# Streaming encoder step, one core: half of w_out reloaded once per tile, two more ring slots for U and two for V

## What is computed

```python
# per layer
x = x + concat([mlstm(q, k, v, gates), sliding_window_attention(q, k, v)]) @ w_out   # w_out: 1024 x 1024
h2 = rmsnorm(x, norm_ffn_w)
x = x + peer(h2)
y = rmsnorm(x, norm_final_w)

def peer(xb):                                   # per row t and head h (8 heads, 16 experts each)
    q  = xb @ w_q                               # 1024 -> 8 heads x 256
    idx, top = best 16 of the 128 x 128 key sums
    g  = softmax(top)
    u  = take(expert_u, idx)                    # 16384 rows of 1024
    a  = gelu(einsum('thkd,td->thk', u, xb))
    ve = take(expert_v, idx)
    return einsum('thk,thkd->td', g * a, ve)
```

## Time and profile before

| | |
|---|---|
| median of 3 runs | 3127.24 us (3126.11 to 3127.49) |
| span of the profiled execution, first to last instruction | 3386.3 us |
| TensorE busy (matrix instructions) | 2600.2 us, 77% |
| VectorE busy | 2120.6 us, 63% |
| GpSimd busy | 1995.2 us, 59% |
| ScalarE busy | 556.3 us, 16% |
| moved by DMA | 1197.02 MB, of it 1107.43 MB by GpSimd's gathers |
| mean granted TensorE clock | 0.811 of full speed |

### The profile page before, as it was taken

One profiled execution on the slowest core, in us unless ns is written; L12 is line 12 of the kernel. 1 busy time (PEld: TensorE's weight loads), 2 busy tenths in 40 slices (PEclk: granted clock), 3 DMA queues, 4 the chain that ended last, 5 costly groups with the idle time before them and its releaser, 6 DMA issues.

```text
span 3386.3 us, 33673 instructions
## 1 busy us (share of the span) xinstructions
PE 2600.2 (77%) x10989; PEld 1007.2 (30%) x10989; DVE 2120.6 (63%) x5282; ACT 556.3 (16%) x1093; POOL 1995.2 (59%) x2128
## 2 busy tenths in 40 slices
PE   8996886678678899987876876678676776686666
PEld 4562351225222533223432331124212331121101
DVE  1256657766676666657667757676667666676653
ACT  2211111211121131122012111111111011111001
POOL 0026556666666566665656666666666666666665
PEclk9997897789677899997987887788667886677667
DMA  6479999999999999999999999999999999999998
GB/s 230 146 275 371 336 338 374 362 371 343 378 351 365 342 400 407 409 382 353 362 329 346 380 354 381 367 364 345 384 360 360 370 365 376 358 368 370 371 363 332
DMA packets 348919, 1197.02 MB, mean 353 GB/s; under 512 B 37760, under 2 KB 54408, under 8 KB 346952
## 3 DMA queue, kind: packets, MB, share of 16 engines
q0 software_dynamic: 304128, 1107.43, 86.7%
q1 hardware_dynamic: 44616, 87.45, 7.0%
HBM read 1180.69 MB, written 14.15 MB: 353 GB/s over the span
## 4 chain that ended last, share of the span: by engine, by line
PE 33%; DVE 16%; issue 13%; POOL 12%; DMA 9%; another core or an unknown queue 8%; DVEq 6%; ACT 1%; ACTq 0%; SPq 0%; POOLq 0%
PE acc L1657 11%; PE mx L1549 7%; DVE ring L1261 7%; POOL ring L593 6%; POOL ring L582 6%; DMA ring<-in_peer_v_dram,idx 5%; DVEq L1148 4%; DMA ring<-in_peer_u_dram,idx 4%; PE mx L1365 3%; PE mx L1531 2%; PE acc L1341 2%; PE mx L1560 2%; PE acc L1328 1%; PE h2p L1603 1%
## 5 line engine op out<-in xcount | busy, mean ns | idle before, releaser
L1657 PE MATMUL acc<-ring,wk 128*32 128x512 f32 x4224 | 1362.6, 742 | 525.6 <-DMA ring<-in_peer_v_dram,idx 289.4
L1261 DVE SCALAR_TENSOR_TENSOR ring<-ring,h2p 128x1024 f32<-128x1024 f32 x1056 | 1273.8, 1215 | 565.4 <-DMA ring<-in_peer_u_dram,idx 315.8
L593 POOL DMA_INDIRECT ring<-in_peer_v_dram,idx x1056 | 997.1, 944 | 707.7 <-issue 269.7
L582 POOL DMA_INDIRECT ring<-in_peer_u_dram,idx x1056 | 996.3, 943 | 667.1 <-issue 292.9
L1657 PEld LDWEIGHTS acc<-ring,wk 128*32 128x32 f32 x4224 | 217.8, 122 | 1406.6 <-issue 670.8
L1549 PE MATMUL mx<-reg,weights 128*128 128x128 f32 x1792 | 256.7, 297 | 40.9 <-issue 38.6
L1549 PEld LDWEIGHTS mx<-reg,weights 128*128 128x128 f32 x1792 | 230.8, 206 | 145.7 <-issue 145.7
L1531 PE MATMUL mx<-weights,reg 128*128 128x512 f32 (+1 forms) x256 | 133.0, 643 | 3.5 <-issue 3.5
L1365 PE MATMUL mx<-weights 128*128 128x512 f32 (+1 forms) x288 | 126.9, 585 | 0.0
L821 ACT ACTIVATE gl<-dots 128x16 f32<-128x16 f32 x66 | 14.2, 216 | 637.5 <-issue 346.1
L1603 PE MATMUL h2p<-ch,ident 32*32 32x512 f32 x528 | 86.7, 708 | 36.6 <-issue 18.9
(11 more groups left out here) (310 smaller groups left out, 2400.3 us busy)
## 6 DMA issues: line engine op xcount, KB each, us to landing
ring<-in_peer_u_dram,idx POOLq DMA_INDIRECT x1056
ring<-in_peer_v_dram,idx POOLq DMA_INDIRECT x1056
weights<-in_peer_w_q_dram SPq DMA_DIRECT2D x7, 2048.0 KB
weights<-in_w_in_dram SPq DMA_DIRECT2D x5, 2048.0 KB, 18.2
weights<-in_w_in_dram SPq DMA_DIRECT2D x10, 1024.0 KB
ring<-in_peer_w_q_dram SPq DMA_DIRECT2D x8, 1024.0 KB, 5.6
xt<-in_x_prompt_dram SPq DMA_DIRECT2D x8, 512.0 KB
ring<-in_w_out_dram SPq DMA_DIRECT2D x2, 2048.0 KB, 14.2
```

The source lines that it names most:

```text
L582: pool.indirect_dma_start(ring[:, n % NU, :], None, u_d, bass.IndirectOffsetOnAxis(ap=idx[:, g % 4, k:k + 1], axis=0)).then_inc(u_in[n % N ...
L593: pool.indirect_dma_start(ring[:, NU + n % NV, :], None, v_d, bass.IndirectOffsetOnAxis(ap=idx[:, g % 4, k:k + 1], axis=0)).then_inc(v_in[ ...
L1261: V.scalar_tensor_tensor(ring[:, n % NU, :], ring[:, n % NU, :], 1.0, h2p[:, :], ALU.mult, ALU.mult, accum_out=dots[:, (g + 1) % 2, k:k + ...
L1657: last = T.matmul(acc[j:j + SUB, cols], wk[:, g % 2, n % TOPK, :], ring[:, NU + n % NV, cols], start=g % 2 == 0 and n % TOPK == 0, stop=g ...
```

## The change

The lower half of `w_out` (row blocks 0 to 3) stays in place. The upper half (blocks 4 to 7, 2 MB) is loaded anew in each of the tiles 1 to 8 by `pass_wout`, into buffers that other steps have finished with: three blocks into `pj` (two) and `reg` (one) once `attn_out` is done, the fourth into `ch` once `cat_transpose` is done. `out_proj` takes blocks 0 to 6 of the left half, then blocks 0 to 6 of the right half, then block 7 of both in its last piece. It waits for the three blocks before its third piece and for the fourth before its last one. The 16 KB on each partition that this frees become ring buffers 6 and 7 of U and 7 and 8 of V. `project_again` waits for the end of tile 3's output projection before its first load, since `reg` is in use until then.

```diff
--- before.py
+++ after.py
@@ -47,8 +47,12 @@
 
 
 SUB = 32
-NU = 6
-NV = 7
+RU, RV = 6, 7
+NU = 8
+NV = 9
+
+
+WK = 4
 GROUPS = 2 * (SEQ // SUB + 1)
 
 
@@ -199,9 +203,12 @@
 
         weights = sb("weights", [P, DC * 2 * PH * NK + DC * D])
         win_s = [weights[:, DC * c0:DC * (c0 + w)].rearrange("p (k c) -> p k c", k=DC) for c0, w in PC]
-        wout_s = weights[:, 0:DC * D].rearrange("p (k c) -> p k c", k=DC)
+        wout_s = weights[:, 0:WK * D].rearrange("p (k c) -> p k c", k=WK)
         wq_s = weights[:, DC * D:].rearrange("p (k c) -> p k c", k=DC)
-        ring = sb("ring", [P, NU + NV, D])
+        ring = sb("ring", [P, RU + RV, D])
+        spare = [weights[:, (WK + i) * D:(WK + i + 1) * D] for i in range(NU - RU + NV - RV)]
+        u_slot = [ring[:, b, :] for b in range(RU)] + spare[:NU - RU]
+        v_slot = [ring[:, RU + b, :] for b in range(RV)] + spare[NU - RU:]
         pj = sb("pj", [P, PJ])
         xt = [sb(f"xt{i}", [P, D]) for i in range(2)]
         ch = [sb(f"ch{i}", [P, D]) for i in range(2)]
@@ -217,6 +224,7 @@
         sm = reg[:, 0:2048].rearrange("p (h s) -> p h s", h=QH)
         t8 = reg[:, 0:1024].rearrange("p (k t) -> p k t", k=DC)
         qrow = reg[:, 1024:1536]
+        wout_pass = [pj[:, 0:D], pj[:, D:2 * D], reg[:, D:2 * D]]
         pT = pj[:, 0:2048].rearrange("p (h b t) -> p h b t", h=QH, b=2)
         qT = pj[:, 0:2048].rearrange("p (c t) -> p c t", c=QC)
         vx = sb("vx", [P, MH, 129])
@@ -289,7 +297,7 @@
         parts_s = room[:, 11520:12032]
         stash = pj[:, 0:QC * NK]
         po = [sc[:, 4 * b:4 * b + 4, :].rearrange("p c k -> p (c k)") for b in range(4)]
-        po += [part[:, :]] + [ring[:, NU + 4, 0:512]] + [a[:, h * 512:h * 512 + 512] for a in (ring[:, NU + 5, :], ring[:, NU + 6, :]) for h in range(2)]
+        po += [part[:, :]] + [ring[:, RU + 4, 0:512]] + [a[:, h * 512:h * 512 + 512] for a in (ring[:, RU + 5, :], ring[:, RU + 6, :]) for h in range(2)]
         first = [pj[:, 0:512], pj[:, 512:1024], vx[:, :, 0:MD], pj[:, 1024:1536], pj[:, 1536:2048], pj[:, 2048:PJ]]
         keys_in = ch[1][:, 0:2 * P]
         mn4 = ch[1][0:MH, 2 * P:3 * P]
@@ -313,6 +321,7 @@
         chunk_act, chunk_dve = sem("chunk_act"), sem("chunk_dve")
         proj_out = [sem(f"proj_out{b}") for b in range(10)]
         wout_in, wq_in = sem("wout_in"), sem("wq_in")
+        wout_pass_in, wout_last_in = sem("wout_pass_in"), sem("wout_last_in")
         keysT_ready, keysT_copied = sem("keysT_ready"), sem("keysT_copied")
         state_in, stateT_ready, state_set = sem("state_in"), sem("stateT_ready"), sem("state_set")
         p_in, x_in = sem("p_in"), sem("x_in")
@@ -436,10 +445,20 @@
                 sp.dma_start(wq_first[j % 4], w_q[0, :, j * 256:j * 256 + 256].rearrange("(k p) c -> p k c", p=P)).then_inc(wq_first_in[j % 4], 16)
 
             def load_wout():
-                sp.dma_start(wout_s, w_out[0].rearrange("(k p) c -> p k c", p=P)).then_inc(wout_in, 16)
+                sp.dma_start(wout_s, w_out[0, 0:WK * P].rearrange("(k p) c -> p k c", p=P)).then_inc(wout_in, 16)
+
+            def pass_wout(m):
+
+                sp.wait_ge(attn_ready, m + 1)
+                for j in range(3):
+                    k = WK + j
+                    sp.dma_start(wout_pass[j], w_out[0, k * P:(k + 1) * P, :]).then_inc(wout_pass_in, 16)
+                sp.wait_ge(rows_transposed, 2 * m + 1)
+                sp.dma_start(ch[m % 2][:, :], w_out[0, (DC - 1) * P:DC * P, :]).then_inc(wout_last_in, 16)
 
             def project_again():
 
+                sp.wait_ge(mixed_ready, FIRST)
                 load_x1_again(FIRST)
                 sp.wait_ge(query_ready, 4 * FIRST)
                 for i in range(2):
@@ -522,6 +541,7 @@
             load_x(1)
             for b in range(10):
                 sp.wait_ge(proj_out[b], stored(b, len(UNITS)))
+            pass_wout(1)
             for m in range(2, TILES):
                 if m == FIRST:
                     project_again()
@@ -539,6 +559,7 @@
                     sp.dma_start(mrow[:, :], st_m[0, 0].rearrange("(h a) -> h a", a=1)).then_inc(state_in, 16)
                 if m != FIRST:
                     load_p(m)
+                pass_wout(m)
                 store_y(m - 2)
                 load_x(m)
             sp.wait_ge(rope_ready, TILES)
@@ -577,9 +598,9 @@
                     pool.wait_ge(topk_done, g + 1)
                 if n >= NU:
                     pool.wait_ge(u_free, n - NU + 1)
-                elif n >= NU - 2:
+                elif RU - 2 <= n < RU:
                     pool.wait_ge(query_ready, 3)
-                pool.indirect_dma_start(ring[:, n % NU, :], None, u_d,
+                pool.indirect_dma_start(u_slot[n % NU], None, u_d,
                                         bass.IndirectOffsetOnAxis(ap=idx[:, g % 4, k:k + 1], axis=0)).then_inc(u_in[n % NU], 16)
 
             def gather_v(g, k):
@@ -587,10 +608,10 @@
                 n = TOPK * g + k
                 if n >= NV:
                     pool.wait_ge(v_free, n - NV + 1)
-                elif n >= NV - 3:
-                    for b in {NV - 3: (5,), NV - 2: (6, 7), NV - 1: (8, 9)}[n]:
+                elif RV - 3 <= n < RV:
+                    for b in {RV - 3: (5,), RV - 2: (6, 7), RV - 1: (8, 9)}[n]:
                         pool.wait_ge(proj_out[b], stored(b, len(UNITS)))
-                pool.indirect_dma_start(ring[:, NU + n % NV, :], None, v_d,
+                pool.indirect_dma_start(v_slot[n % NV], None, v_d,
                                         bass.IndirectOffsetOnAxis(ap=idx[:, g % 4, k:k + 1], axis=0)).then_inc(v_in[n % NV], 16)
 
             for k in range(TOPK):
@@ -1258,7 +1279,7 @@
                     if k == 0 and g % 2:
                         dve.wait_ge(h2p_set, (g + 1) // 2 + 1)
                     dve.wait_ge(u_in[n % NU], 16 * (n // NU + 1))
-                    V.scalar_tensor_tensor(ring[:, n % NU, :], ring[:, n % NU, :], 1.0, h2p[:, :], ALU.mult, ALU.mult,
+                    V.scalar_tensor_tensor(u_slot[n % NU], u_slot[n % NU], 1.0, h2p[:, :], ALU.mult, ALU.mult,
                                            accum_out=dots[:, (g + 1) % 2, k:k + 1]).then_inc(u_free, 1)
                     if k == TOPK - 1:
                         dve.drain().then_inc(dots_done, 1)
@@ -1518,16 +1539,28 @@
                     for k in range(DC):
                         T.matmul(mx[0:n, k // 4, k % 4 * P:(k % 4 + 1) * P], ident[0:DC, k:k + 1].broadcast_to([DC, n]), ffw[0:DC, :], start=True, stop=True)
                 elif s == "out_proj":
-                    half, k0 = i // 4, i % 4 * 2
+                    pairs = [(i // 4, i % 4 * 2 + a) for a in range(2)]
+                    if m > 0:
+                        pairs = [divmod(2 * i + a, DC - 1) for a in range(2)] if i < DC - 1 else [(0, DC - 1), (1, DC - 1)]
                     if i == 0:
                         if m >= 2:
                             pe.wait_ge(y_ready, m - 1)
                         if m == 1:
                             pe.wait_ge(wout_in, 16)
                     if m == 0 and i % 4 == 0:
-                        pe.wait_ge(wout_first_in[half], 16)
-                    for k in (k0, k0 + 1):
-                        w = wout_first[half][:, k, :] if m == 0 else wout_s[:, k, half * 512:half * 512 + 512]
+                        pe.wait_ge(wout_first_in[i // 4], 16)
+                    if m > 0 and i == WK // 2:
+                        pe.wait_ge(wout_pass_in, 16 * 3 * m)
+                    if m > 0 and i == DC - 1:
+                        pe.wait_ge(wout_last_in, 16 * m)
+                    for half, k in pairs:
+                        cols = slice(half * 512, half * 512 + 512)
+                        if m == 0:
+                            w = wout_first[half][:, k, :]
+                        elif k < WK:
+                            w = wout_s[:, k, cols]
+                        else:
+                            w = (wout_pass + [ch[m % 2][:, :]])[k - WK][:, cols]
                         last = T.matmul(mx[0:n, 2 + half, :], t8[:, k, 0:n], w, start=k == 0, stop=k == DC - 1)
                     if i == 7:
                         last.then_inc(mixed_ready, 1)
@@ -1654,7 +1687,7 @@
                             pe.wait_ge(v_in[n % NV], 16 * (n // NV + 1))
                             for half in range(2):
                                 cols, j = slice(half * 512, half * 512 + 512), (g // 2 + 2 * half) % 4 * SUB
-                                last = T.matmul(acc[j:j + SUB, cols], wk[:, g % 2, n % TOPK, :], ring[:, NU + n % NV, cols],
+                                last = T.matmul(acc[j:j + SUB, cols], wk[:, g % 2, n % TOPK, :], v_slot[n % NV][:, cols],
                                                 start=g % 2 == 0 and n % TOPK == 0, stop=g % 2 == 1 and k == TOPK - 1)
                             last.then_inc(v_free, 1)
                     for s, i, m in steps.get(t, ()):
```

## The result

The changed kernel takes 3154.51 us (median of 4 runs, 3151.73 to 3156.58); the kernel before took 3126.68 us beside it. The ratio is 1.0088, 95% interval [1.0074, 1.0103]: 0.9% slower, where 0.8% faster was forecast.

A forecast was written before the change was run, and what follows sets the result against it. GpSimd, which issues the gathers, stood at full rings, leaving the DMA engines short of 409 GB/s. 3127.24 us - 46 (deeper rings) + 20 (reloads) + 0 (due times) = 3101 us; range 3065 to 3155 us.

The forecast's parts named there:

- rival 1: Whole kernel: DMA engines are the limit, rings only add waiting gathers, loads show in full, up to 3168 us; chance 0.18.
- rival 1's signs: In the gathers: GpSimd's waits fall, time from issue to landing grows, rate stays at 366 to 380 GB/s.
- The shortfall: After the first 200 us, timed runs lose 93 us against moving their bytes at 409 GB/s, the most rings can win.
- Part 1: U and V gather rings: two slots more in each win half of the 93 us, 46 us; bounds 0 and 93 us.
- Part 2: Reloads of w_out before the output projection: half of their 41 us shows, 20 us slower; bounds 0 and 41 us.
- Part 3: Due times of the w_out loads: out_proj waits for none, cost 0; with twice the landing time 20 us in tile 4.
- rival 3: Output projection: a late w_out block, landing times double and TensorE stands waiting, 3177 us; chance 0.06.
- Rival 2: Query and projection slots: TensorE paces them, ring waits only move, load bursts fall into slack, 3127 us; chance 0.13.
- Rival 4: Gather rings: the reserve wins more, ceiling above 409 GB/s or bursts vanish in slack, 75 us off, 3052 us; chance 0.10.
- the four signs for the forecast: GpSimd's V waits fall a quarter or more, tile window above 366 GB/s, TensorE's 289 us wait falls, no out_proj load wait.
- the range of 8 in 10: Whole kernel's time: expected with 8 in 10 chances between 3065 and 3155 us.
- The lower ceiling: DMA rate: by the skill's limit of about 358 GB/s no shortfall is left, and the sum would be 3174 us.

The follow-up runs named there:

- e1: Changed kernel with rings back at 6 (U) and 7 (V), so the reload alone: 3162.65 us, ratio 1.0115 to the kernel before.
- e2: Changed kernel with the reload and its waits taken out, rings of 8 and 9 alone: 3114.08 us, ratio 0.9963 to the kernel before.
- e0: The kernel before, unedited, timed and profiled once more: 3127.3 us, ratio 0.9999, profiled span 3125.3 us.
- e3: Changed kernel with every block of the reload loaded twice, 16.8 MB more again: 3195.05 us, ratio 1.0219 to the kernel before.
- e8: The changed kernel, unedited, timed again: 3151.87 us, ratio 1.0081 to the kernel before at 3126.12 us.
- e11: Kernel before with only the U ring deeper (rings of 8 and 7, no reload): 3124.92 us, ratio 0.9993.
- e4: Kernel before with V gathers of 2 KB a row instead of 4 KB: 3409.13 us, ratio 0.9957 to the kernel before at 3420.66 us.
- e6: Kernel before with only the U ring deeper (rings of 8 and 7, no reload): 3392.39 us, ratio 0.9912 to the kernel before at 3420.66 us.
- e7: Changed kernel with two of eight w_out blocks reloaded and rings of 6 and 9: 3510.22 us, ratio 1.0249 to the kernel before at 3420.66 us.
- e9: Kernel before with V gathers of 2 KB a row, timed where the kernel before takes 3126.12 us: 2971.97 us, ratio 0.9509.
- e5: Kernel before with only the V ring deeper (rings of 6 and 9, no reload): 3510.78 us, ratio 1.0250 to 3420.66 us.
- e10: Kernel before with only the V ring deeper (6 and 9, no reload), timed where the kernel before takes 3126.12 us: 3120.12 us, ratio 0.9981.

## Why the prediction was wrong

**The result is near rival 1's.** That one said up to 3168 us, if the loads show in full and the rings win nothing. Measured one by one: reload +35 to +36 us (e1), rings -12 to -14 us (e2), together +21 to +24 us against a measured +26 to +28 us. The bytes tell it more closely. Take from each page's bytes those of the first 200 us (190 GB/s in e0, 178 to 180 in the others): what then lacks to 409 GB/s is a shortfall of about 92 us in e0, 86 us in e1, 76 us in e2, 76 us in the changed kernel and 75 us in e3. So the changed kernel pays some 42 us for bytes and gets 15 us back from gaps; a second reload gets almost nothing more. Its mean after the start is 398 GB/s, under the 402 that rival 1 named as the bound. Of rival 1's signs, the longer time to landing came (12.0 to 17.5 us); the rate of 366 to 380 GB/s did not.

**The shortfall, the step that failed.** The size, 93 us, was right; that rings could win half of it was not. I took the form of the waits from an execution 259 us longer than the timed ones, and scaled it down. In a timed run the shortfall isn't a thinner form of those waits. Two thirds of it sit at the start of the gathers, from 920 to 1640 and at the end (e0's windows). The rings close 9 us of it behind the start and nearly all of it in some steady tiles (403 to 408 GB/s from 2000 to 2340), and little elsewhere (e2's windows): 15 us of 92. The prediction had the warning in its own numbers: 1159.2 MB in 2927 us are 396 GB/s, 97% of the ceiling, over a stretch that takes in such weak parts. Rival 1 said so and got 0.18; where the time of the profiled execution and of the runs differ by 8%, an argument from the runs' own time and bytes should have weighed more than the waits of the trace.

**Part 1 (46 us; 12 to 14 measured).** This is the larger miss, some 33 of the 54 us between forecast and result. The half came from capping eight chains of waits in a tile. In e0 GpSimd's waits for V are 142 us and not 414 us. And by this account a wait of GpSimd costs nothing while gathers are queued before the DMA engines: 12 us from issue to landing are nine gathers of 1.28 us. That V slots matter more than U slots was right (6 us against 1 us), that they bring nearly all of the gain was not: two V slots alone bring half of what the four bring together.

**Part 2 (20 us; 36 measured, 41 for the second load).** The other 16 us or more. I counted slots in which TensorE is slower than the two gathers as slack. That slack exists only if the DMA engines then stand still, and they hardly do: they fill the rings. e0's whole-tile windows leave 5 to 8 us each, e1's reload fills 5 or 6 us of them in all eight tiles together, and e3 shows that after the first reload nothing is left.

**Part 3 (0) was right.** The landings of the reloads in the changed kernel, KB each and median us:

```profile
pj<-in_w_out_dram SPq DMA_DIRECT2D x16, 512.0 KB, 8.5
...
reg<-in_w_out_dram SPq DMA_DIRECT2D x8, 512.0 KB, 11.5
ch<-in_w_out_dram SPq DMA_DIRECT2D x8, 512.0 KB, 6.8
```

The third block lands 11.5 us after its issue, within the 20 us that tile 4 leaves. What the output projection's line waited for:

```profile
  issue: 97.3, 231
  DVEq L1256: 1.1, 1
```

No DMA is among it, so rival 3 falls. The first load, halved, brought nothing that shows (e1). Rival 2 falls with e1 and e3, which show the loads nearly in full. Rival 4 counted on a ceiling above 409 GB/s or on bursts that vanish; no window or slice shown here passes 410, and e1 and e3 show the bursts.

**The signs, and the number.** Of the four signs for the forecast three came: GpSimd's waits for V fell by more than a quarter, the tile's window moved more than 366 GB/s, and no out_proj piece waited on a load. The first two came because they were measured against the slower execution: e0 has them without the change (142 us, 403 GB/s). The fourth, a fall of TensorE's 289 us, did not come: 361.3 + 97.9 = 459 us in the changed kernel, 454.4 in e0. That 3154.51 us is still inside the range of 8 in 10, which ends at 3155 with half of the loads hidden, is luck: the loads were hidden to a small part only, and the rings won 12 to 14 us against them. And a third more or less of each term gives 3079 to 3123 us, not the 3080 to 3118 that the prediction gave as its own range.

**The lower ceiling.** The Trainium skill ("DMA: Bandwidth & Descriptors", Specifications) puts the HBM limit of one core at about 358 GB/s. Its part on bandwidth gives that figure for both cores of an HBM domain streaming, and here one core works. The direction that follows from the limit, a kernel whose bytes set its time, was right; the figure doesn't hold for this case: e0 moves 403 GB/s over a tile, and e3's second load goes at 16.8 MB in 40.5 us, 414 GB/s.

## What to carry to other kernels

Before paying bytes for buffers, divide the bytes by the time of the timed runs: at 97% of the best rate that any window shows, a deeper ring mostly lengthens the queue, and each added MB costs nearly its full time (2.4 us here). Even free of charge, the four slots were worth 0.4%. If the profiled span and the timed median differ by more than a per cent, the waits in that trace are another run's waits: read the rates that both share, and take another profile if one can be had. Where two rings are filled in turn, deepen both or expect the waits to move to the other one.

## What was not expected of the hardware

The same kernel took 3120 to 3134 us in the sets with e0 to e3 and e8 to e11 and 3405 to 3433 us in the one with e4 to e7, steadily within each. In the latter the bytes are no limit (e4: 0.4% for 277 MB, against 4.9% in e9), the size of one ring moves the time by 2.5% (e5) or 0.9% the other way (e6), and the chain puts 8% to 15% on releases that the profile can't name. The cause stays open. The busy share of the DMA engines is of little use for telling the two conditions apart: 0.97 at 366 GB/s, 1.02 at 403 GB/s. One of e10's ten executions took 9432.62 us, at a granted clock of 1.0 where the others had 0.84; no trace shows it, and its cause is open too.
